# Recurrent heads in a two-layer decoder step: all level products beside the diagonal, key and value transposes side by side

## What is computed

```
def step(S, inp):
    qc, kc, vc, lc = inp
    G = jnp.cumsum(lc, axis=2)
    diff = G[:, :, :, None, :] - G[:, :, None, :, :]
    decay = jnp.exp(jnp.where(causal[:, :, None], diff, -jnp.inf))
    A = jnp.einsum('bhtd,bhsd,bhtsd->bhts', qc, kc, decay)
    o = jnp.einsum('bhts,bhse->bhte', A, vc) + jnp.einsum('bhtd,bhde->bhte', qc * jnp.exp(G), S)
    Gl = G[:, :, -1]
    S = jnp.exp(Gl)[..., None] * S + jnp.einsum('bhsd,bhse->bhde', kc * jnp.exp(Gl[:, :, None] - G), vc)
    return S, o
```

## Time and profile before

| what | value |
|---|---|
| median of three runs | 1330.16 us (1329.25 to 1330.41) |
| the profiled execution: its time, its span | 1329.18 us, 1327.2 us |
| TensorE busy | 1309.9 us, 99% of the span |
| VectorE, ScalarE, GpSimd busy | 801.1, 595.8, 188.8 us |
| stage of the recurrent heads | about 618 to 876 us of the span |

### The profile page before, as it was taken

The page is one execution under the profiler, slowest core; times in us unless marked ns, Lnnn a source line. Parts: engine busy times, 40 slices in busy tenths (PEclk is TensorE's granted clock), DMA queues, the critical chain, the costliest instruction groups (busy, mean ns, idle before and its releaser), DMA issues.

```text
span 1327.2 us, 32854 instructions
## 1 busy us (share of the span) xinstructions
PE 1309.9 (99%) x13100; PEld 1279.8 (96%) x13100; DVE 801.1 (60%) x1457; ACT 595.8 (45%) x1207; POOL 188.8 (14%) x321
## 2 busy tenths in 40 slices
PE   9999999999999999999999999999999999999997
PEld 8998999999999999997999999999999999999996
DVE  6476476655566632238988888967665665552224
ACT  5367355333333322237666666646433333332231
POOL 0111221111111100000211111211111111110000
PEclk9999999999999999999999999999999999999999
DMA  8312321223222322212333333341222222342211
GB/s 293 115 50 65 96 94 51 94 81 95 83 91 79 124 88 88 81 60 83 110 112 97 97 97 101 98 140 50 62 85 92 95 79 85 95 125 88 89 41 68
DMA packets 39686, 123.24 MB, mean 93 GB/s; under 512 B 4232, under 2 KB 12168, under 8 KB 39496
## 3 DMA queue, kind: packets, MB, share of 16 engines
q1 hardware_dynamic: 35400, 111.92, 26.7%
q10 hardware_dynamic: 4048, 10.00, 2.3%
q0 software_dynamic: 176, 0.44, 0.1%
HBM read 113.78 MB, written 8.57 MB: 92 GB/s over the span
## 4 chain that ended last, share of the span: by engine, by line
PE 93%; DVE 3%; ACT 1%; issue 1%; DMA 0%; SPq 0%; DVEq 0%; ACTq 0%
PE acc L449 87%; PE aux L606 1%; PE aux L753 1%; PE aux L628 1%; PE aux L781 0%; PE aux L737 0%; DVE x L1593 0%; PE aux L618 0%; PE aux L776 0%; DVE mix L1588 0%; DMA x<-in_xT 0%; DVE h_lo L1380 0%; PE aux L527 0%; DVE w_lo L1371 0%; PE aux L545 0%
## 5 line engine op out<-in xcount | busy, mean ns | idle before, releaser
L1371 DVE TENSOR_TENSOR w_lo<-raw,w_hi 128x512 fp32r<-128x512 f32 (+1 forms) x372 | 305.7, 825 | 322.9 <-ACT w_hi L883 322.7
L449 PE MATMUL acc<-h_hi,w_hi 128*128 128x272 f32 x2208 | 474.4, 292 | 3.5 <-DVE h_lo L1380 2.9
L449 PE MATMUL acc<-h_hi,w_lo 128*128 128x272 f32 x2208 | 464.7, 288 | 0.0
L449 PE MATMUL acc<-h_lo,w_hi 128*128 128x272 f32 x2208 | 463.2, 288 | 0.0
L449 PEld LDWEIGHTS acc<-h_hi,w_hi 128*128 128x128 f32 x2208 | 349.6, 188 | 15.9 <-issue 7.6
L883 ACT CAST w_hi<-raw 128x512 fp32r<-128x512 f32 (+1 forms) x372 | 236.4, 642 | 273.3 <-PE acc L449 268.0
L449 PEld LDWEIGHTS acc<-h_lo,w_hi 128*128 128x128 f32 x2208 | 349.9, 188 | 0.2
L449 PEld LDWEIGHTS acc<-h_hi,w_lo 128*128 128x128 f32 x2208 | 347.9, 189 | 0.0
L449 PE MATMUL acc<-g_hi,w_hi 128*128 128x272 f32 x704 | 153.1, 288 | 0.0
L449 PE MATMUL acc<-g_hi,w_lo 128*128 128x272 f32 x704 | 153.0, 289 | 0.0
L449 PE MATMUL acc<-g_lo,w_hi 128*128 128x272 f32 x704 | 152.3, 288 | 0.0
(11 more groups left out here) (256 smaller groups left out, 1343.4 us busy)
## 6 DMA issues: line engine op xcount, KB each, us to landing
raw<-in_w_up SPq DMA_DIRECT2D x88, 512.0 KB, 3.6
raw<-in_w_down SPq DMA_DIRECT2D x32, 704.0 KB, 4.1
raw<-in_w_in_c SPq DMA_DIRECT2D x32, 512.0 KB, 3.6
raw<-in_w_in_ab SPq DMA_DIRECT2D x18, 512.0 KB, 3.9
raw<-in_w_out_ab SPq DMA_DIRECT2D x8, 512.0 KB, 3.6
S<-in_state ACTq DMA_DIRECT2D x8, 512.0 KB, 3.7
o_ss<-Snew ACTq DMA_DIRECT2D x8, 512.0 KB, 2.7
raw<-in_w_out_c SPq DMA_DIRECT2D x8, 512.0 KB, 3.6
```

The source lines that it names most:

```text
L449: mm = pe.matmul(acc[out][:, t, 0:H], w[slot][:, wc], mv[:, kk_, t * H:(t + 1) * H], start=start and k == 0 and q == 0, stop=stop and k == ...
L1371: dve.tensor_tensor(w_lo[slot][:, to], raw[n % 4][:, cols], w_hi[slot][:, to], ALU.subtract).then_inc(lo_ready, 1)
```

## The change

On TensorE the three levels move from t = 1 to t = 0. That visit now runs level 1, the samples, the diagonal, levels 2 and 3, and the state updates, and waits for `lev_ready` at its start. The visit at t = 1 is gone. The transposes of the keys move from t = 5 to t = 6, ahead of those of the values. ScalarE's copies of the keys move from its t = 5 to its t = 6, VectorE's `kdT_lo` from t = 5 to t = 6. The diagonal and the second and third level share bank A[1] and get other columns in it, and VectorE masks the samples first and the diagonal after them, once all products are there.

```diff
-                            to, lhs = P * (which - 2) + 32 * (n // 4) + 16 * (n % 2), lev[which - 1][:, block]
+                            to, lhs = P * which + 32 * (n // 4) + 16 * (n % 2), lev[which - 1][:, block]
...
                         pe.wait_ge(C["kdT_copied"], prev + 1)
-                        levels(prev, 0)
+                        pe.wait_ge(C["lev_ready"], LEVELS * prev + LEVELS)
+                        levels(prev, 1)
                         pe.wait_ge(C["v_hi"], prev + 1)
                         pe.matmul(A[3][0:NB * TS, 0:NB * TS], E2[:, TP:T], E1[:, TP:T], start=True, stop=True
                                   ).then_inc(C["al_done"], 1)
+                        for which in (0, 2, 3):
+                            levels(prev, which)
...
-                    if t == 1:
-                        pe.wait_ge(C["lev_ready"], LEVELS * prev + LEVELS)
-                        pe.wait_ge(C["al_taken"], 4 * prev + 2)
-                        for which in range(1, 1 + LEVELS):
-                            levels(prev, which)
...
-                    if t == (6 if prev is None else 5):
+                    if t == 6:
                         pe.wait_ge(C["kd_ready"], cur + 1)
...
-                    act.wait_ge(C["al_done"], 5 * prev + 3)
+                    act.wait_ge(C["al_done"], 5 * prev + 2)
...
-                    if t == 5:
+                    if t == 6:
                         act.wait_ge(C["kdT_done"], cur + 1)
                         act.copy(kt[:].rearrange("p a b -> p (a b)"), A[0][:])
...
-                dve.wait_ge(C["al_done"], 5 * prev + (5 if which else 1))
+                dve.wait_ge(C["al_done"], 5 * prev + 5)
...
-                        take_level(prev, 0)
                         dve.wait_ge(C["al_done"], 5 * prev + 2)
                         came(3, 5)
                         dve.copy_predicated(AT_s[R0, :], mask_s[:], A[3][0:NB * TS, 0:NB * TS]).then_inc(C["al_taken"], 1)
+                        take_level(prev, 0)
                         states(prev)
...
                             level_ops(2, cur)
-                            kdT_lo(cur)
...
                     if prev is None:
-                        kdT_lo(cur)
                         level_ops(2, cur)
                     level_q(0, cur)
                 if t == 6:
                     level_q(1, cur)
+                    kdT_lo(cur)
                     dve.wait_ge(C["v_hi"], cur + 1)
```

More of the change, by code:

```diff
@@ L1830, in take_level @@
                     at = later(AT[:], span).rearrange("p (c n) s -> p c n s", c=NBLK)
-                    al = A[1][:, P * (which - 2):P * (which - 1)].rearrange("p (c n s) -> p c n s", c=NBLK, s=span)
+                    al = A[1][:, P * which:P * (which + 1)].rearrange("p (c n s) -> p c n s", c=NBLK, s=span)
                     mask = later(masks[:, which, :], span).rearrange("p (c n) s -> p c n s", c=1)
```

## The result

The changed kernel takes 1351.41 us (median of 6 runs, 1350.24 to 1353.89) against 1330.14 us: a ratio of 1.0162, 95% interval 1.0152 to 1.0172. It is slower, as forecast, but by 21.3 us where 15.3 had been worked out, and it lies 3.4 us above the range. The profiled execution took 1351.39 us, with a span of 1349.3 us.

A forecast was written before the change was run, and what follows sets the result against it. TensorE, busy 1309.9 of 1327.2 us, bounds the kernel; a new 33.43 us loop through VectorE sets the pace. The last level product ends 13.2 us later, plus 2.1 for chunk states: 1329.18 + 15.3 = 1344.5 us, range 1336 to 1348.

The forecast's parts named there:

- First S, 639.08: First head: VectorE ends its last level product, and the merged visit at t = 0 can start, at 639.08 us.
- The loop, 33.43 us: From one head's end of VectorE's last level product to the next: 33.43 us, where TensorE alone needs 31.63.
- term of 1.0 us for the key copies: ScalarE's moved key copies stand ahead of the value copies VectorE waits for, adding 1.0 us to each loop.
- a wait buys no lead: Each head waits 1.8 us at t = 0; the rival, only the first wait paid, 1331.0 us, had chance 0.06.
- The saving, 0.20 us a head: TensorE's way in and out of the level visit at t = 1 goes: 0.20 us in each of eight heads.
- The last loop, 34.71 us: Last head: longer stretch from the eviction of f to the last level product's end; loop 34.71 us, ending at 874.37.
- the 3 that I named: Expected TensorE wait at the last merged visit, line 727 for line 1760: about 3 us (34.71 less 31.63).
- The clock: Rival: TensorE's clock falls behind the first wait, costing 3.0 us as one half at half speed; 1347.5 us, chance 0.08.
- the sum: Main case over all heads: 13.2 us later last level product plus 2.1 us of states, 1344.5 us, chance 0.70.
- one of my signs of being wrong: Profile after: TensorE's clock below full behind the first wait would show the prediction wrong.
- GpSimd's collision: Rival: VectorE's w_lo (1.91 us against 0.69) no longer meets GpSimd's line 2092; 8.5 us less, 1336 us, chance 0.06.

The follow-up runs named there:

- the kernel with both ways cut: Changed kernel with key transposes and copies back at t = 5 and VectorE's last level product ahead of its wait for the values: 1331.15 us, ratio 1.0007.
- the run with 28 and 20: Changed kernel plus 28 extra matmuls ahead of the half before the first visit at t = 0 and 20 ahead of the last visit: 1348.19 us, ratio 1.0139.

## Why the prediction was wrong

- *First S, 639.08.* Held: the visit starts at 639.12.
- *The loop, 33.43 us.* Held: 33.22. Its term of 1.0 us for the key copies was measured, with the transposes and the low half moved along, as 33.22 − 32.21 = 1.0. That a wait buys no lead held as well: the steady wait is 1.6 us in every head.
- *The saving, 0.20 us a head.* A little more: 31.83 − 31.54 = 0.29 us, in the kernel with both ways cut.
- *The last loop, 34.71 us.* Held: 34.72. The wait in it is 4.6 us and not the 3 that I named: TensorE's own work between the last two visits is only 30.08 us (829.63 to 859.71 in the kernel with both ways cut), and I had taken 31.63. The kernel before had shown it: its last visit starts at 857.92, 30.33 us after the one at 827.59.
- *The clock: the step that failed.* I priced its fall at 3.0 us behind one wait, and gave it 0.08 as a rival, although the sum itself held a wait of 4 us and no row showed the clock full through more than 1.5. So the sum had it at nothing; it cost 3.0 us in the first loop and 1.6 behind the last visit, and a clock below full behind the first wait, one of my signs of being wrong, came. That the price of 3.0 fits is partly luck: it was meant as one whole half at half speed, and it is 2.0 us in the visit and 1.1 in the first part of the half, in a visit that the issue wait had stretched (2.1 us without that). Behind the last visit the clock is at half as well, and the updates and the first part of the half run slow there: from the visit's start to L767 it takes 886.67 − 878.58 = 8.1 us, where the sum has 6.5 (the same matmuls began at 865.62 in the kernel before; 865.62 + 15.3 − 874.37), 1.6 us more. In the run with 28 and 20, at full clock, it takes 6.35 (876.65 to 883.00).

```profile
886.67 0.63 PE L767 MATMUL aux<-vbd,kt_s 96*128 96x512 f32 x2
```

  By the rule of the Trainium skill, "TensorE: Matmul & The Clock Gate", section "Part 1: The HAM clock gate", an array that idles drops to 1.2 GHz; the trace agrees, 0.50 behind the waits of 4.2 and 4.6 us, while those of 1.6 us left the clock at 1.00. (Waits of 2.2 and 2.5 us in two of the experiments were followed by 0.50 too.) I should have put it into the sum wherever a wait was longer than the rows vouched for.
- *What no step held: the issue wait.* 2.3 us in the first visit and 1.0 at L779 in the last head (the kernel before has one of 0.7 us at L791, at 650 us, in the first pass of the loop, and none in the last head). The merged visit runs 89 short matmuls in a row (178 rows), and in its first pass TensorE stops at a certain place of them. That it goes with the place is shown; that instructions arrive late is likely from the packets, and not shown.
- *GpSimd's collision stays.* Right. But I had read one head for seven. In the kernel before, w_lo is the long row in two heads (660.58 and 819.01), and in the other five it is the multiplication behind it, 1.88 us against 0.72:

```profile
724.11 1.88 DVE L1891 TENSOR_TENSOR scratch<-scratch,c_sg 128x544 f32<-128x544 f32 x1
```

  After the change it is w_lo once (667.76) and the multiplication six times, each beside GpSimd's line 2089:

```profile
833.88 0.69 DVE L1369 TENSOR_TENSOR w_lo<-raw,w_hi 128x512 fp32r<-128x512 f32 x1 [0.53 <-ACT w_hi L881]
834.49 1.87 DVE L1889 TENSOR_TENSOR scratch<-scratch,c_sg 128x544 f32<-128x544 f32 x1
```

```profile
833.91 1.87 POOL L2089 TENSOR_TENSOR c_qG<-c_eG,c_qn 128x544 f32<-128x544 f32 x1
```

The account: 1344.5, plus 5.2 for the first loop (38.65 less 33.43), less 1.05 for five loops of 0.21, plus 1.6 for the last visit and its half, makes 1350.3. The other 1.1 us of the profiled execution are the outputs of the last head: from L767 to the next half it takes 4.13 us (886.67 to 890.80), for 2.95 in the kernel before (865.62 to 868.57), with the issue wait of 1.0 us in between. Behind that the two kernels take the same time.

## What to carry to other kernels

When a visit on the busiest engine is moved ahead, list every way by which its end leads back to its next start, and cut all of them: here each half of the change closed one, and cutting the longer alone only showed the other. When a sum contains a new TensorE wait longer than any that the trace shows at full clock, put the half clock into the sum and not among the rivals. When short matmuls are put together, look in their first pass for a wait without a releaser; a few extra instructions ahead show whether it goes with the place. And read a price from the rows of the stretch itself: a loop time that comes out as expected can hold something else.

## What had not been expected of the hardware

- TensorE stopped for 1.4 to 3.3 us (six kernels) in the middle of 89 short matmuls, in code that runs for the first time (the first pass of the loop, or the visit behind the loop), with nothing in the profile that it waited for; 9 tiny matmuls ahead of it were enough to take the stop of 2.3 us out of the first visit, while 18 and 12 larger ones put one into the last (3.32 us).
- A stop of that kind was followed by a fall of the clock like any other wait: behind 3.21 us of it, from full clock and a busy array, the clock was at 0.50 for two microseconds and more.
- The 64 tiny matmuls of ones stand as 128 rows in the trace and took 4.2 us, 33 ns a row, where 63 rows of level products of the same shape run in 0.76 us, 12 ns a row. The tiny ones all write the same 32 rows of one bank, the level products four groups of rows in turn; whether that is the reason was not tried.
